# The last conv FFN: gate and up tiles in seven half-size products, with weight sums on GpSimd and a convolution that reads SBUF

## The reference, cut to what matters

```
def dwconv_grid(h, w, b, grid):            # 3 x 3, one filter for each feature
    img = h.reshape(bn, rows, width, F)
    out = lax.conv_general_dilated(img, w[:, :, None, :], (1, 1), "SAME", feature_group_count=F)
    return out.reshape(bn, L, F) + b

def conv_ffn(h, w_up, conv_w, conv_b, w_down, grid):
    gate, up = jnp.split(h @ w_up, 2, axis=-1)
    gate = dwconv_grid(gate, conv_w, conv_b, grid)
    return (jax.nn.gelu(gate, approximate=True) * up) @ w_down

    xl = xl + mod_l[5] * rmsnorm(conv_ffn(hl, ffn_w_up[layer], ...), norm_g[layer, 3])
```

## Time and profile before

| | us |
|---|---|
| median of 3 runs (lowest, highest) | 3435.51 (3429.36, 3435.82) |
| time of the profiled execution | 3436.1 |
| its span, first to last instruction | 3434.3 |
| gate and up of the last block, from its first matmul | 3188.8 to 3342.9 |
| its down projection | 3344.9 to 3422.8 |

### The profile page before, as it was taken

How to read it: one execution, slowest core, us unless ns; L and a number is a source line. 1 busy time by engine, 2 the same in 40 slices (tenths; PEclk the granted TensorE clock), 3 DMA queues, 4 the chain that set the end, 5 groups by cost and what they waited for, 6 DMA issues and landing times. The chain is left out here.

```text
span 3434.3 us, 54420 instructions
## 1 busy us (share of the span) xinstructions
PE 3189.5 (93%) x24210; PEld 1926.6 (56%) x24210; DVE 995.1 (29%) x2185; ACT 593.8 (17%) x1336; POOL 225.3 (7%) x198
## 2 busy tenths in 40 slices
PE   7999996899999999989988999999898888888998
PEld 4788784633323332254765544444544777777887
DVE  0255115311100110023064233420313555461560
ACT  1010012210000000032144200000202343432100
POOL 0000000000000000000032100000000223131000
PEclk9999998899999999979989899999798989998999
DMA  9778841169988889922002133333211000004340
GB/s 365 280 281 326 326 176 65 56 265 377 377 352 344 341 360 376 390 77 74 2 1 98 49 123 146 119 127 121 80 50 58 14 21 17 14 3 180 120 155 13
DMA packets 88492, 577.04 MB, mean 168 GB/s; under 512 B 9536, under 2 KB 15936, under 8 KB 20672
## 3 DMA queue, kind: packets, MB, share of 16 engines
q1 hardware_dynamic: 84800, 568.27, 42.4%
q10 hardware_dynamic: 3456, 5.24, 0.4%
HBM read 567.19 MB, written 6.29 MB: 167 GB/s over the span
## 5 line engine op out<-in xcount | busy, mean ns | idle before, releaser
L267 PE MATMUL ps<-H,ring 128*128 128x256 f32 (+1 forms) x2928 | 909.4, 473 | 19.3 <-ACT H L557 8.9
L267 PEld LDWEIGHTS ps<-H,ring 128*128 128x128 f32 x2928 | 567.4, 195 | 361.1 <-issue 309.5
L267 PE MATMUL ps<-W,ring 128*128 128x256 f32 (+1 forms) x1488 | 470.3, 477 | 11.3 <-DVE W L2858 8.0
L1706 PE MATMUL ps<-ring,W 128*32 128x512 f32 (+1 forms) x2816 | 474.1, 596 | 1.7 <-ACT H L1766 1.7
L267 PEld LDWEIGHTS ps<-W,ring 128*128 128x128 f32 x1488 | 284.6, 193 | 199.2 <-issue 172.3
L1706 PEld LDWEIGHTS ps<-ring,W 128*32 128x32 f32 (+1 forms) x2816 | 136.6, 123 | 288.1 <-issue 285.5
L1730 PE MATMUL ps<-ring,W 128*64 128x512 f32 (+1 forms) x1408 | 240.1, 598 | 0.0
L1988 DVE SCALAR_TENSOR_TENSOR W<-ps,vec,W 128x189 f32<-128x189 f32 (+3 forms) x396 | 173.3, 438 | 14.0
L1730 PEld LDWEIGHTS ps<-ring,W 128*64 128x64 f32 (+1 forms) x1408 | 65.0, 123 | 169.3 <-issue 169.3
L3383 POOL TENSOR_TENSOR ring<-ring 128x512 f32<-128x512 f32 x96 | 124.5, 1315 | 529.7 <-DVE ring L3407 461.8
L1814 DVE TENSOR_TENSOR H<-ps,H 128x256 f32<-128x256 f32 x66 | 28.0, 424 | 358.0 <-ACT H L1757 358.0
(11 more groups left out here) (427 smaller groups left out, 3130.0 us busy)
## 6 DMA issues: line engine op xcount, KB each, us to landing
ring<-weights SPq DMA_DIRECT2D x528, 1024.0 KB, 7.1
rkv<-W ACTq DMA_DIRECT2D x16, 256.0 KB, 2.0
ring<-rkv SPq DMA_DIRECT2D x8, 512.0 KB, 3.7
X<-tokens SPq DMA_DIRECT2D x2, 1024.0 KB, 8.6
ring<-rw_tiles SPq DMA_DIRECT2D x8, 256.0 KB, 2.7
rkv<-W ACTq DMA_DIRECT2D x8, 128.0 KB, 2.1
ring<-rkv SPq DMA_DIRECT2D x8, 128.0 KB, 3.7
out<-X SPq DMA_DIRECT2D x8, 128.0 KB, 1.9
```

The source lines that it names most:

```text
L267: mm = pe.matmul(out(o), lhsT=k.ring[:, k.slot(at), p * P:(p + 1) * P], rhs=rhs(kk), start=kk == 0, stop=kk == kt - 1)
L1706: mm = pe.matmul(ps[at:at + n, r, :], lhsT=moe.Hg[:, kt, FIRST * e + first:FIRST * e + first + n], rhs=w[e][:, kk * WIDE:(kk + 1) * WIDE], ...
```

## The change

Only the last block changes. `stage_last_ffn` takes the place of `stage_conv_ffn` there. Unit 0 is computed as before, into banks 6 and 7. Units 1 to 21 go by `Seven`. The four sums of each unit are made by GpSimd, which has them in its list ahead of `rms.add`. ScalarE copies P1 (x1), copies P1 + P2 (the first token half of the gate) to `firsts` in SBUF, and makes the GELU of unit u - 1. VectorE makes C12 into the other half of `firsts`, and convolves unit u - 1 out of `firsts` while TensorE is at unit u: five steps, then `early` of unit u, then the other four, then the product of unit u - 2, then `late` of unit u. After unit 21 come the product of 20, the whole convolution of 21 and the product of 21. `Seven.sums` and the names of two outputs are made settable for that; nothing changes in `stage_swiglu`.

```diff
+        self.made = k.dve
+        self.top = lambda u: self.c12[u % 2]
+        self.bottom = lambda u: self.up[u % 2]
...
-    def sums(self, dve, u):
-        k, S, done = self.k, self.S[u % 2], self.done
+    def sums(self, eng, u):
+        k, S, done, made = self.k, self.S[u % 2], self.done, self.made
...
+        eng.wait_ge(k.w_in[k.slot(place)], k.landed(place))
         if u >= 3:
+            self.product_done(eng, u - 2, self.P3)
+        eng.tensor_tensor(S[:, 0, :], A(2, 1), A(2, 2), ALU.add).then_inc(made.sem, 1)
...
+def stage_last_ffn(k, Y, pre, rms):
+    seven = Seven(k, p, k.H[:, :, cols], n, KF * n, done)
+    seven.made = k.pool
+    firsts = [k.W[:, at:at + n] for at in (14080, 14848)]
+    seconds = seven.up + [k.W[:, 15104:15360]]
+    seven.top = lambda u: firsts[u % 2][:, h:n]
+    seven.bottom = lambda u: seconds[u % 3]
...
+            def sums_done(u):
+                pe.wait_ge(k.pool.sem, k.pool.at(done["S4", u]))
+                if u == 1:
+                    pe.wait_ge(k.dve.sem, k.dve.at(done["T4", 0]))
+            for u in range(1, KF):
+                seven.products(pe, u, first_free, sums_done)
...
+            def taps(f):
+                y, x = conv[:, f % 2, 0:n], firsts[f % 2] if f else k.ps[:, 6, 0:n]
+                if f:
+                    dve.wait_ge(k.act.sem, k.act.at(done["first", f]))
+                    dve.wait_ge(k.dve.sem, k.dve.at(done["C12", f]))
...
+                link(dve.tensor_scalar(y, x, w(1, 1), k.v("fcb", layer * KF + f), ALU.mult, ALU.add))
+                yield
...
+                    ins = dve.scalar_tensor_tensor(yo, xg[:, r0 + a:r1 + a, c0 + b:c1 + b], w(a + 1, b + 1), yo, ALU.mult, ALU.add)
...
+            seven.tokens(dve)
+            for u in range(1, KF):
+                convolution = taps(u - 1)
+                for _ in range(5):
+                    next(convolution)
+                seven.early(dve, u)
+                for _ in convolution:
+                    pass
+                if u > 1:
+                    gated(u - 2)
+                seven.late(dve, u)
+            gated(KF - 2)
+            for _ in taps(KF - 1):
+                pass
+            gated(KF - 1)
...
+        def _(pool):
+            pre.pool(pool)
+            pre.ready(pool, KD - 1)
+            for u in range(1, KF):
+                seven.sums(pool, u)
+            rms.add(pool)
...
+            for u in range(1, KF):
+                seven.copy_first(act, u)
+                seven.product_done(act, u, seven.P2)
+                if u > 2:
+                    act.wait_ge(k.dve.sem, k.dve.at(done["conv", u - 2]))
+                act.activation(firsts[u % 2][:, 0:h], seven.bank(seven.FIRST), ACT.Copy).then_inc(k.act.sem, 1)
+                gelu(u - 1)
...
-    stage_conv_ffn(k, 1, LAT, Y, Several(), pre, rms)
+    stage_last_ffn(k, Y, pre, rms)
```

More of the change, by code:

```diff
@@ L900, in tokens @@
         dve.tensor_tensor(T[4], B(2, 1), T[2], ALU.subtract).then_inc(k.dve.sem, 1)
-    def sums(self, dve, u):
-        k, S, done = self.k, self.S[u % 2], self.done
+    def sums(self, eng, u):
+        k, S, done, made = self.k, self.S[u % 2], self.done, self.made
         A = self.quarter(u)
         place = self.plan.at(u)
-        dve.wait_ge(k.w_in[k.slot(place)], k.landed(place))
+        eng.wait_ge(k.w_in[k.slot(place)], k.landed(place))
         if u >= 3:
[L908 to L914, removed]
+            self.product_done(eng, u - 2, self.P3)
+        eng.tensor_tensor(S[:, 0, :], A(2, 1), A(2, 2), ALU.add).then_inc(made.sem, 1)
+        eng.tensor_tensor(S[:, 2, :], A(1, 1), A(2, 1), ALU.subtract).then_inc(made.sem, 1)
+        eng.wait_ge(made.sem, made.at(done["S1", u]))
+        eng.tensor_tensor(S[:, 1, :], S[:, 0, :], A(1, 1), ALU.subtract).then_inc(made.sem, 1)
+        eng.wait_ge(made.sem, made.at(done["S2", u]))
+        eng.tensor_tensor(S[:, 3, :], A(1, 2), S[:, 1, :], ALU.subtract).then_inc(made.sem, 1)
     def early(self, dve, u):
@@ L926, in early @@
         self.product_done(dve, u, self.P5)
-        dve.tensor_tensor(self.up[u % 2][:, h:2 * h], self.bank(self.FIFTH), self.u3[u % 2], ALU.add).then_inc(k.dve.sem, 1)
+        dve.tensor_tensor(self.bottom(u)[:, h:2 * h], self.bank(self.FIFTH), self.u3[u % 2], ALU.add).then_inc(k.dve.sem, 1)
     def late(self, dve, u):
@@ L932, in late @@
         self.product_done(dve, u, self.P4)
-        dve.tensor_tensor(self.up[u % 2][:, 0:h], self.bank(self.SEVENTH), self.u2[u % 2], ALU.add).then_inc(k.dve.sem, 1)
+        dve.tensor_tensor(self.bottom(u)[:, 0:h], self.bank(self.SEVENTH), self.u2[u % 2], ALU.add).then_inc(k.dve.sem, 1)
         self.product_done(dve, u, self.P3)
-        dve.tensor_tensor(self.c12[u % 2], self.bank(self.FIFTH), self.u2[u % 2], ALU.add).then_inc(k.dve.sem, 1)
+        dve.tensor_tensor(self.top(u), self.bank(self.FIFTH), self.u2[u % 2], ALU.add).then_inc(k.dve.sem, 1)
 def stage_swiglu(k, i, ada, pre, rms, finishes):
@@ L2022, in stage_conv_ffn, with _, first_free, before_down @@
     k.dve.base += 2 * KF
+    k.unit += len(p.order)
+def stage_last_ffn(k, Y, pre, rms):
+    nc = k.nc
+    n, h, cols, layer = S, S // 2, LAT, 1
+    A = k.W[:, 0:KF * n].rearrange("p (o t) -> p o t", o=KF)
+    conv = k.W[:, 15360:15360 + 2 * T].rearrange("p (b t) -> p b t", b=2)
+    p = Plan([t // KD for t in range(2 * KF * KD)] + [2 * KF + t // KF for t in range(KD * KF)], seven=KF)
+    unit_done, out_done, signals, total = p.unit_done, p.out_done, p.signals, p.total
+    down0 = 2 * KF
+    rows = n // GRID_W
+    gate = Gate(k, layer, 1, cols)
+    done = {("C21", 0): 4, ("C12", 0): 4}
+    for i, name in enumerate(("T1", "T3", "T2", "T4")):
+        done[name, 0] = i + 1
+    dves = 4
+    for u in range(1, KF):
+        for name, v in [("U2", u), ("U3", u), ("C22", u), ("conv", u - 1)] + [("A", u - 2)] * (u > 1) + [("C21", u), ("C12", u)]:
+            dves += 1
+            done[name, v] = dves
+        for i, name in enumerate(("S1", "S3", "S2", "S4")):
+            done[name, u] = 4 * u - 3 + i
+        done["x1", u], done["first", u], done["gelu", u - 1] = 3 * u - 2, 3 * u - 1, 3 * u
+    done["A", KF - 2], done["conv", KF - 1], done["A", KF - 1] = dves + 1, dves + 2, dves + 3
+    dves += 3
+    acts = done["gelu", KF - 1] = 3 * KF - 2
+    seven = Seven(k, p, k.H[:, :, cols], n, KF * n, done)
[4 more added lines that the diff above has]
+    seven.bottom = lambda u: seconds[u % 3]
+    with nc.Block() as block:
+        @block.sync
+        def _(sp):
+            refill(k, sp, unit_done, len(p.order))
+        @block.tensor
+        def _(pe):
+            pre.tensor(pe)
+            gemm(k, pe, 2, KD, lambda kk: k.H[:, kk, cols], lambda o: k.ps[:, 6 + o, 0:n], lambda o: None, signals,
+                 plan=p, ready=pre.ready)
+            def first_free(u):
+                if u > 1:
+                    pe.wait_ge(k.act.sem, k.act.at(done["first", u - 1]))
+            def sums_done(u):
[4 more added lines that the diff above has]
+                seven.products(pe, u, first_free, sums_done)
+            def before_down(o):
+                pe.wait_ge(k.dve.sem, k.dve.at(dves))
+                if o >= 4:
+                    pe.wait_ge(k.act.sem, k.act.at(acts + o - 3))
+            gemm(k, pe, 8, KF, lambda kk: A[:, kk, :], lambda o: k.ps[:, o % 4, 0:n], before_down,
+                 signals, first=down0 * KD, plan=p)
+        @block.vector
+        def _(dve):
+            pre.vector(dve)
+            gate.vector(dve)
+            link = Link(k.dvel, dve)
+            def taps(f):
+                y, x = conv[:, f % 2, 0:n], firsts[f % 2] if f else k.ps[:, 6, 0:n]
+                w = lambda a, b: k.v("fcw", layer * 9 * KF + (3 * a + b) * KF + f)
+                if f:
+                    dve.wait_ge(k.act.sem, k.act.at(done["first", f]))
+                    dve.wait_ge(k.dve.sem, k.dve.at(done["C12", f]))
+                else:
+                    dve.wait_ge(k.mm.sem, k.mm.at(out_done[0]))
+                if f >= 2:
+                    dve.wait_ge(k.dve.sem, k.dve.at(done["A", f - 2]))
+                link(dve.tensor_scalar(y, x, w(1, 1), k.v("fcb", layer * KF + f), ALU.mult, ALU.add))
+                yield
+                yg, xg = y.rearrange("p (r c) -> p r c", r=rows), x.rearrange("p (r c) -> p r c", r=rows)
+                places = [(a, b) for a in (-1, 0, 1) for b in (-1, 0, 1) if (a, b) != (0, 0)]
+                for a, b in places:
+                    r0, r1 = max(0, -a), rows - max(0, a)
+                    c0, c1 = max(0, -b), GRID_W - max(0, b)
+                    yo = yg[:, r0:r1, c0:c1]
+                    ins = dve.scalar_tensor_tensor(yo, xg[:, r0 + a:r1 + a, c0 + b:c1 + b], w(a + 1, b + 1), yo, ALU.mult, ALU.add)
+                    if (a, b) == places[-1]:
+                        ins.then_inc(k.dve.sem, 1)
+                    else:
+                        link(ins)
+                    yield
+            def gated(f):
```

(38 more changed lines are left out.)

## The result

The changed kernel takes 3486.18 us as median (3485.28 to 3491.61), the kernel before 3432.88 (3429.36 to 3435.82) in the same comparison: 1.0161 times as long, with a 95% interval of 1.0147 to 1.0175. That is some 53 us slower. The profiled execution has a span of 3484.4 us, against 3434.3.

What follows compares the result with a forecast made beforehand. TensorE bounded the kernel before, VectorE taking turns with GpSimd after: 6.7 + 19 x 9.35 - 1.2 + 6.3 + 6.4 = 195.9 against 147.1 us, +48.8, plus 2 for the clock: 3486 us, range 3450 to 3510.

Steps and rivals of the forecast that it cites:

- The bound: Gate and up stage: TensorE alone sets the pace before the change; seven products take 6.25 us a unit against 6.91.
- VectorE's own list: VectorE's steps in one unit with nobody in its way: 5.79 us, under TensorE's 6.25.
- The first step: The convolution's `tensor_scalar` from SBUF: 0.353 us plus 0.03 to the next, against 0.54 from PSUM.
- The turns: GpSimd's sums and VectorE steps with two SBUF inputs alternate: 3.5 us lost a unit, making it about 9.35.
- the first working: Loss a unit from GpSimd's 4.88 us, less 0.52 for C21 and C12 and 0.88 around reading: 3.5, unit 9.3.
- the prediction's second working: Loss a unit from four held steps at 1.516 - 0.485 = 1.03 us, less 0.52: 3.6, unit 9.4.
- The clock: TensorE's clock in the stage: short falls hidden because VectorE is the bound; 2 us added to the total.
- VectorE without waits: Sign expected in the changed kernel's profile: VectorE never waits in a unit of 9.3 us.
- Start and end: Unit 1 about 6.7 us, units 2 and 3 some 0.6 less than later ones, end gap 6.3 to 6.4.
- No contention: Rival: sums are free, TensorE bounds units at 6.25 to 6.44 us; 9.5 faster, 3426; chance 0.08.
- Half the contention: Rival: GpSimd's sums meet the product, C21, C12 and U2 to C22; unit 7.5 us, 3449; chance 0.10.
- The clock's rival: Rival: TensorE's clock falls with its 3 us gaps; a third of units at half clock, +20 us, 3506; chance 0.10.

Runs made afterwards that it cites:

- the two runs without turns: Changed kernel with GpSimd's sums of units 3 to 21 one column wide: 3421.22 us; changed kernel with full sums and the gate (firsts) in PSUM: 3421.89 us.
- the sums cut: Changed kernel with GpSimd's four sums of units 3 to 21 made one column wide: 3421.22 us, 0.9968 of the kernel before.
- the run with fillers: Changed kernel with eight matmuls of unread result ahead of P4 in each unit of the last block: 3478.38 us, 1.0131 of the kernel before.
- The half dose: Changed kernel with GpSimd's sums of units 3 to 21 cut to 256 of 512 columns: 3438.48 us, 1.0016 of the kernel before.

## Why the prediction was right, point by point

**The bound.** Right. TensorE set the pace, 0.66 us a unit were there to be had, and the two runs without turns got them: 9.3 and 9.2 us less for the stage, against a forecast of 9.5. The seven products take 6.25 us in each (P1 at 3279.89 and 3286.14 with the sums cut).

**VectorE's own list.** Forecast at 5.79 us, 5.83 measured with the sums on VectorE. The first step was 0.41 and not 0.353; all other terms together came out within 0.1.

**The turns.** Right in kind: the place, the steps that are held, and GpSimd's 1.3 to 1.4. The size was forecast at 3.5 us a unit and is 8.87 - 5.83 = 3.04 with the clock at full. The count of four held steps was right: in the run with fillers the sums begin beside C21 and C12, hold `tensor_scalar` for 0.79 - 0.41 = 0.38, and three of the four taps behind it for 4.50 - 1.83 = 2.67 together. The product was never among them (0.426 us at most, in all 21). The term that was too large is the price of one held step. I took 1.03 from a row in which the tap began 0.04 us behind the GpSimd operation and waited for nearly all of it, and 1.22 - 0.25 = 0.97 in the first working; here the next sum is 0.23 us old when the tap begins (3313.98 and 3314.21), and a held tap costs 1.30 - 0.415 = 0.89. With that the prediction's second working gives 4 x 0.89 - 0.52 = 3.04.

**The clock.** Wrong as a term. I called its falls hidden and put 2 us down for them. Its chain is the one I left out: P4 and P3 come behind TensorE's gap, and C12, at which VectorE's list turns, waits for P3. In the change VectorE waited there 0.34 to 1.15 us in 12 of the 21 units, against the prediction's sign "VectorE without waits", and units were 8.86 to 10.5 us long (P4 at 3216.38, 3225.24, and 3368.21, 3378.68). The mean of units 3 to 20 is (3382.07 - 3209.37) / 18 = 9.59, so that at the full clock these 18 units would be 18 x 0.72 = 13 us shorter. The fillers took 10.3 us off the stage and 7.8 off the median, though all they do is add work, and with them the clock is at 1.00. They give back less than 13 because units 1 and 21, where TensorE has no gap to fill, became 1.6 and 1.8 us longer. A fast P3 also starts the sums earlier, beside C21 and C12, which is part of the same gain (`tensor_scalar` held for 0.38 in place of 0.73).

So 9.35 stood against 9.59, and it was the sum of a term 0.5 too large and another 0.7 too small. That the forecast of 3486 came out at 3486.18 is luck in two ways. The two errors offset each other in part, and the 2 us for the clock covered part of the rest. And the forecast rise was 50.5 us on a median of 3435.5, where the measured one is 53.3 on 3432.88, with the stage 54.2 longer.

**Start and end.** Unit 1 took 7.17 us (6.7 forecast; T4 came 0.68 late, a loss that was given as up to 0.5). Units 2 and 3 took 9.61 and 8.90; the 1.2 us that they were to save together against the later ones (mean 9.59) came to 0.7. The gap at the end was 5.78 us (6.3 to 6.4 forecast). The errors of unit 1 and of the gap all but cancel.

**The rivals.** No contention is what the change would be without the second SBUF input: 3421 to 3423, where I had 3426; as a gain that is 9 to 11 us against 9.5. Half the contention did not come: each of the four sums held a step that reads SBUF alone, and none fell on the PSUM steps only. The half dose (7.04 a unit, 3438) is no test of it, since it makes the sums shorter and moves none of them. The clock's rival was right in that the clock falls with the gaps and costs time. Its size, 20 us, compares with the 13 above, and its way was another: not whole units at half the clock, but P4 and P3, which hold up C12.

**The rule of the Trainium skill.** "SBUF — State Buffer", "Who interferes with whom", says that the pair of ports is held exclusively, by whoever issues first, and that an instruction with one SBUF input outside the two-port modes is not concerned. By that rule, the traces agree: a step held ends 0.2 us behind the sum that held it (rows above), and with x in PSUM nothing is held (1.83 us for four taps). The section also names `tensor_scalar` among the operations that can enter a two-port mode and can then contend. By that, the trace agrees here too: from SBUF to SBUF it was held in the change (1.128 us as median, 0.408 at the least), with one tensor input only.

## What to carry to other kernels

Before work is handed to an idle GpSimd, look at where the inputs of VectorE's instructions of that stretch lie: with two in SBUF (or a `tensor_scalar` from SBUF to SBUF), and a GpSimd instruction that reads SBUF, the two engines run one after the other, and the work that was handed over is not hidden. Four sums on GpSimd cost VectorE 3.04 us a unit here, and 2.53 when it made them itself. An input left in PSUM, or put there, makes both free. Here that took two banks, and 0.13 us more for the `tensor_scalar` (0.54 in place of 0.41). And a gap that TensorE gets in every round can cost time of its own, when what the others wait for comes right behind it at half the clock: some 13 us over 18 units here.

## What was not expected of the hardware

TensorE stood for 1.5 to 2.4 us ahead of P4 in each of units 2 to 20 of the change, and its granted clock was at 0.90 over the stage; with waits of 0.52 to 0.57 us at the same place (half width, fillers) it was 1.00. Whether a unit met the half clock varied: in some P4 and P3 took 0.9 to 1.0 us each, in others up to 1.9 and 1.7. The gap ahead of P4 was as long in units of the one kind as of the other (2.34 us ahead of 3225.24 and of 3337.14), so what decides for a single unit stays open. Eight more matmuls a unit, 168 in all, shortened the program by 7.8 us.
